# Moving three elementwise jobs of a state-space layer from GpSimd to VectorE, and one convolution tap to ScalarE

## The reference

```
zxbcdt = rms_norm(h, norm_w) @ in_w
z, xbc, dt = split(zxbcdt, [2048, 2048 + 3072])
xbc = silu(causal depthwise conv of 4 taps(xbc) + conv_b)
xs, bm, cm = split(xbc)                      # 32 heads of 64; 4 groups of state 128
dt = softplus(dt + dt_bias);  a_cum = cumsum(dt * a) within chunks of 128
y = sum_j (c_i . b_j) * exp(a_cum_i - a_cum_j) * x_j * dt_j   (j <= i)
y = (y + d_skip * xs) * silu(z)
y = group_norm(y) * gnorm_w @ out_w
```

## Time and profile before

| | |
|---|---|
| median of 3 runs | 1514.42 us (1511.16 to 1514.44) |
| the profiled execution | 1517.64 us, its span 1515.8 us |
| TensorE busy | 1302.9 us (86%), 9346 products |
| VectorE busy | 784.4 us (52%) |
| ScalarE busy | 558.1 us (37%) |
| GpSimd busy | 159.3 us (11%) |
| mean granted TensorE clock | 0.885 of full speed |
| chain that ended last | TensorE 69%, VectorE 11%, DMA 6%, ScalarE 6% |

### The profile page before, as it was taken

The page is one execution under the profiler, slowest core; times in us unless marked ns, Lnnn a source line. Parts: engine busy times, 40 slices in busy tenths (PEclk is TensorE's granted clock), DMA queues, the critical chain, the costliest instruction groups (busy, mean ns, idle before and its releaser), DMA issues.

```text
span 1515.8 us, 21867 instructions
## 1 busy us (share of the span) xinstructions
PE 1302.9 (86%) x9346; PEld 1156.6 (76%) x9346; DVE 784.4 (52%) x1328; ACT 558.1 (37%) x884; POOL 159.3 (11%) x121
## 2 busy tenths in 40 slices
PE   5899697799989998974858999978879888886797
PEld 4787376688868887973848999978867688775697
DVE  0178112944444446480526664358976554547544
ACT  2221513111110005121425553354456754476635
POOL 0101000000000000000000000116635300031000
PEclk8999798889979999556879999979999889899888
DMA  9977478547655454289543555613433234342131
GB/s 302 338 244 254 134 139 248 170 171 271 247 184 176 167 184 156 95 161 233 179 120 125 191 185 183 193 57 114 136 101 95 84 113 137 111 139 84 56 113 55
DMA packets 207029, 244.39 MB, mean 161 GB/s; under 512 B 30596, under 2 KB 191572, under 8 KB 202708
## 3 DMA queue, kind: packets, MB, share of 16 engines
q1 hardware_dynamic: 191752, 183.08, 40.2%
q0 software_dynamic: 10880, 41.95, 8.1%
q10 hardware_dynamic: 4300, 17.96, 3.0%
HBM read 224.16 MB, written 18.81 MB: 160 GB/s over the span
## 4 chain that ended last, share of the span: by engine, by line
PE 69%; DVE 11%; DMA 6%; ACT 6%; SPq 4%; issue 3%; POOL 0%; ACTq 0%; DVEq 0%
PE ps L1256 18%; PE ps L1249 10%; PE ps L1251 9%; PE ps L1253 9%; PE ps L1549 4%; PE ps L1481 3%; PE ps L1304 2%; PE ps L1334 2%; DVE ada_w L2303 2%; DMA ring<-in_w_fc 2%; DMA ring<-k_dram 2%; PE ps L1277 1%; PE ps L1485 1%; PE ps L1462 1%; SPq L664 1%
## 5 line engine op out<-in xcount | busy, mean ns | idle before, releaser
L1249 PE MATMUL ps<-sq_rounded,w_high 128*128 128x256 f32 x960 | 282.6, 294 | 28.7 <-DVE hT_rounded L1846 12.1
L1253 PE MATMUL ps<-sq_rounded,ring_rounded 128*128 128x256 f32 x960 | 275.4, 287 | 0.0
L1839 DVE TENSOR_TENSOR ring_rounded<-ring,w_high 128x1024 fp32r<-128x1024 f32 x152 | 186.7, 1270 | 102.0 <-ACT w_high L800 101.9
L1251 PE MATMUL ps<-hT_rounded,w_high 128*128 128x256 f32 x832 | 239.2, 288 | 0.0
L800 ACT ACTIVATE w_high<-ring 128x1024 fp32r<-128x1024 f32 x176 | 176.0, 1048 | 118.2 <-PE ps L1253 97.2
L1249 PEld LDWEIGHTS ps<-sq_rounded,w_high 128*128 128x128 f32 x960 | 188.8, 197 | 37.5 <-issue 33.2
L1256 PE MATMUL ps<-hT,ring 128*128 128x256 f32 x832 | 193.5, 392 | 7.7 <-DMA ring<-in_w_fc 6.1
L1256 PEld LDWEIGHTS ps<-hT,ring 128*128 128x128 f32 x832 | 161.6, 197 | 38.0 <-issue 15.2
L1253 PEld LDWEIGHTS ps<-sq_rounded,ring_rounded 128*128 128x128 f32 x960 | 188.7, 197 | 0.0
L1251 PEld LDWEIGHTS ps<-hT_rounded,w_high 128*128 128x128 f32 x832 | 164.4, 198 | 0.2
L1249 PE MATMUL ps<-more_rounded,w_high 128*128 128x256 f32 x448 | 126.3, 282 | 0.7 <-issue 0.7
(11 more groups left out here) (378 smaller groups left out, 2047.6 us busy)
## 6 DMA issues: line engine op xcount, KB each, us to landing
ring<-in_w_fc SPq DMA_DIRECT2D x64, 1024.0 KB, 5.4
ada_w<-in_ada_w POOLq DMA_DIRECT2D x27, 1024.0 KB, 7.4
ring<-in_ssm_in_w SPq DMA_DIRECT2D x20, 1024.0 KB, 5.3
ada_more<-in_ada_w POOLq DMA_DIRECT2D x13, 1024.0 KB, 7.6
ring<-in_w_in SPq DMA_DIRECT2D x12, 1024.0 KB, 8.3
we_dram<-we_t ACTq DMA_DIRECT2D x8, 1024.0 KB, 3.9
ca_dram<-more ACTq DMA_DIRECT2D x8, 1024.0 KB, 6.0
ring<-we_dram SPq DMA_DIRECT2D x8, 1024.0 KB, 4.8
```

What stands on the lines that cost most here:

```text
L1249: nc.tensor.matmul(out, high[:, k, columns], x_high, start=start, stop=False, skip_group_check=True)
L1251: nc.tensor.matmul(out, high[:, k, columns], x_low, start=False, stop=False, skip_group_check=True)
L1253: last = nc.tensor.matmul(out, low[:, k, columns], x_high, start=False, stop=stop, skip_group_check=True)
L1839: nc.vector.tensor_tensor(rounded(w), w, w_high[:, c % 2, ks], ALU.subtract)\
```

## The change

- `SPLIT_LO` has VectorE make the low parts of xbc as well. They are placed in VectorE's queue: block 0 ahead of the norm of the layer, block m+1 ahead of `convolve(m)`, z_0 so ahead of `convolve(11)`. At unit 0 the place is behind the wait for the dt products.
- The tap that needs no shift (tap 3) goes to ScalarE: two instructions per unit read PSUM, multiply by the tap and write `convolved`, between the copy into `padded` and the signal `xbc_copied`. VectorE's `convolve` then has three taps, six multiply-adds on `convolved`.
- `weigh` and the gate move to VectorE. weigh(0) and weigh(1) stand ahead of the loop; in iteration t the order is: low part of z_(t/2+1) where t is even, skip(t), segments(t+2), gate(t), and for 1 <= t < 15 weigh(t+1).
- GpSimd keeps only the transfers of the modulation weights and the swaps in the attention layer.

```diff
-SPLIT_LO = {"glu": "vector", "fc1_1": "vector", "fc2_1": "vector", "xbc": "gpsimd", "z": "vector",
+SPLIT_LO = {"glu": "vector", "fc1_1": "vector", "fc2_1": "vector", "xbc": "vector", "z": "vector",
...
-            for b in split_order:
-                if split_low[b][0] == "gpsimd":
-                    for half in range(2):
-                        pool.wait_ge(w_high_ready, 2 * split_place[b] + half + 1)
...
-            weigh(0)
-            weigh(1)
-            for t in range(Z_TILES):
-                pool.wait_ge(zs_ready, t // 2 + 1)
-                pool.wait_ge(y_skipped, t + 1)
-                nc.gpsimd.tensor_tensor(xs[:, t], xs[:, t], zs[:, t], ALU.mult).then_inc(y_gated, 1)
-                if t + 2 < Z_TILES:
-                    weigh(t + 2)
...
-                nc.scalar.activation(padded[:, m % 4].rearrange("p (k n) -> p k n", k=2)[:, :, 3:3 + T], ps,
-                                     ACT.Copy).then_inc(xbc_copied, 1)
+                nc.scalar.activation(padded[:, m % 4].rearrange("p (k n) -> p k n", k=2)[:, :, 3:3 + T], ps, ACT.Copy)
+                if m >= 2:
+                    act.wait_ge(xbc_ready, m - 1)
+                for i in range(2):
+                    tile = 16 + 2 * m + i if m < 4 else 2 * (m - 4) + i
+                    ins = nc.scalar.activation(convolved[:, m % 2, T * i:T * i + T], ps[:, i], ACT.Copy,
+                                               scale=col("ssm_conv_w_2", 72 + tile))
+                ins.then_inc(xbc_copied, 1)
...
+            lower_to(first_block["xbc"] + 1)
             split_norm(5, "ssm_norm_w_2", "xbc")
...
-                for tap in range(4):
+                for tap in range(3):
...
+                lower_to(first_block["xbc"] + m + 2)
                 convolve(m)
...
+            def weigh(t):
+
+                dve.wait_ge(seg_exp, t + 1)
+                s = seg[:, t % 2]
+                nc.vector.tensor_tensor(s, s, cb[:, t // 4].unsqueeze(1).to_broadcast([P, 2, SEG]), ALU.mult)\
+                    .then_inc(seg_weighed, 1)
...
             weigh_by_dt(6)
             weigh_by_dt(7)
+            dve.wait_ge(cb_ready, SSM_GROUPS)
+            weigh(0)
+            weigh(1)
             for t in range(Z_TILES):
...
                 if t + 2 < Z_TILES:
                     segments(t + 2)
+                dve.wait_ge(y_skipped, t + 1)
+                dve.wait_ge(zs_ready, t // 2 + 1)
+                nc.vector.tensor_tensor(xs[:, t], xs[:, t], zs[:, t], ALU.mult).then_inc(y_gated, 1)
+                if 1 <= t < Z_TILES - 1:
+                    weigh(t + 1)
```

More of the change, by code:

```diff
@@ L192, in split_plan @@
     starts = sorted((b, name) for name, b in first_block.items())
-    counts = {"vector": 0, "gpsimd": 0}
+    counts = {"vector": 0}
     for i, (start, name) in enumerate(starts):
@@ L199, in split_plan @@
             counts[SPLIT_LO[name]] += 1
-            low[b] = (SPLIT_LO[name], counts[SPLIT_LO[name]])
+            low[b] = counts[SPLIT_LO[name]]
     return order, place, low
@@ L299, in program @@
         w_low_vector = sem("w_low_vector")
-        w_low_gpsimd = sem("w_low_gpsimd")
         a_high = sem("a_high")
@@ L1240, in block_products @@
                     if split and k // 4 == waited:
-                        engine, count = split_low[b]
-                        pe.wait_ge(w_low_vector if engine == "vector" else w_low_gpsimd, 2 * count - 1 + waited)
+                        pe.wait_ge(w_low_vector, 2 * split_low[b] - 1 + waited)
                         waited += 1
@@ L1834, in lower_to @@
                     b = split_order[c]
-                    for half in range(2) if split_low[b][0] == "vector" else ():
+                    for half in range(2):
                         dve.wait_ge(w_high_ready, 2 * c + half + 1)
@@ L2290, in convolve @@
                 dve.wait_ge(xbc_copied, m + 1)
-                if m >= 2:
-                    dve.wait_ge(xbc_ready, m - 1)
                 src = padded[:, m % 4].rearrange("p (k n) -> p k n", k=2)
-                for tap in range(4):
+                for tap in range(3):
                     for i in range(2):
@@ L2298, in convolve @@
                         dst = convolved[:, m % 2, T * i:T * i + T]
[L2299 to L2302, removed]
+                        if tap:
+                            behind(1)
                         ins = nc.vector.scalar_tensor_tensor(out=dst, in0=src[:, i, tap:tap + T], scalar=w, in1=dst,
                                                              op0=ALU.mult, op1=ALU.add)
-                        if tap == 3 and i == 1:
+                        if tap == 2 and i == 1:
                             ins.then_inc(xbc_conv, 1)
```

## The result

The changed kernel takes 1529.8 us (median of 4 runs, 1527.5 to 1532.1) against 1514.4 us before; the ratio is 1.0109, its 95% interval 1.0084 to 1.0133. It is slower by 15 us, where 1527 us were forecast. The profiled execution took 1529.9 us, its span 1528.0. One more execution of the kernel before took 2132.6 us; it does not enter the ratio.

The account below looks back on a forecast made before the run. Ahead of z1 TensorE waits on VectorE and GpSimd; the z loop has no idle time. Terms -9.0 (xbc stage) -6.7 (up to z1) +16.3 (z-loop wait) +12.5 (clock) = +13.1 us on 1514.4: 1527 us, range 1511 to 1537.

Parts of the forecast that it names:

- dt products to block 3: Start of the xbc stage: VectorE's first low halves come later, so block 3 starts at about 1040.4, against 1039.1.
- block 3 to X: Rest of the xbc stage, X being block 11's end: blocks follow one another, 55.7 us for blocks 3 to 11.
- X to z_1, without the clock: From block 11's end to z1: the 5.8 us wait for z0's low half goes; gain 6.7 us (5 to 8).
- z loop, the wait: Second contraction at S+4.65, not S+1.86 (S: even contraction's start); 2.8 us more per pair, loss 16.3 us (12 to 20).
- z loop and first pair, the clock: TensorE's clock falls to 1.2 GHz in nearly every z pair; loss 12.5 us (0 to 18).
- some 4 us cold, 2 us lost: Each clock fall in a z pair: some 4 us at the low clock, costing half of that busy time, 2 us.
- Rival 1: Clock stays at 2.4 GHz in the z pairs; sum +0.6, 1515 us; chance 0.17.
- The row at 1166.2: Profile row before the change: clock at 1.2 GHz from 1166.2 although TensorE had idled only some 0.4 us.
- Rival 2: Wait before the second contraction shorter (2.0 us a pair), clock kept; sum -7, 1507 us; chance 0.10.
- Rival 3: VectorE bounds the xbc stage too, so the gain there is 4 to 5 us; 1532 us; chance 0.11.
- the signs named beforehand: Include xbc unit ends 5.7 to 5.9 us apart, seven 2.7 us weighing waits, z pairs 12 to 15 us, clock near 0.8.

Follow-up runs that it names:

- six fillers: Changed kernel plus six unused 256-column products on TensorE in each of six waits before an odd contraction (blocks z_1 to z_6); 1516.5 us, ratio 1.0027.

## Why the prediction was right, step by step

The steps by the traces, with the forecast beside them:

| step | forecast | measured | from |
|---|---|---|---|
| dt products to block 3 | +1.3 | +0.9 | 27.9 - 27.0 |
| block 3 to X | -10.3 | -11.2 | 55.5 - 66.7 |
| X to z_1, without the clock | -6.7 | -6.9 | 16.9 - 21.7, less 2.1 |
| z loop, the wait | +16.3 | +15.7 | six fillers against before, 18.3 - 2.6 |
| z loop and first pair, the clock | +12.5 | +19.9 | 15.2 + 2.6 + 2.1 |
| sum | +13.1 | +18.5 | 226.8 - 208.3 |

**The xbc stage** went as worked out. TensorE waited 2.04 us for block 1, where 2.0 were expected between the dt products and 1020.8, and 2.67 us for block 2. Taps cost 0.83 us where 0.85 was taken, the loop stayed under TensorE's pace, and blocks followed one another without a gap. 10.3 us were won by X, 9.0 forecast; the slack of 0.6 us I had kept for weighing by dt wasn't needed. Between block 3 and X the kernel before has 5.8 us of waits and 7.4 us at 1.2 GHz, the changed kernel neither: part of what moving the low halves won is clock as well.

**Up to z_1.** contract(0) starts at X+11.1 in the trace, as forecast to the tenth. The pair behind it took 5.8 us instead of 3.7, because the clock fell in it; that is the 2.1 us counted with the clock (1.7 forecast). The wait of 5.8 us for z_0's low part is gone, as said.

**The wait in the z loop** was right in its mechanism and its size: the second contraction at S+4.62 (S+4.65 forecast), 2.69 us idle in six pairs and 1.92 in the last. The weighing takes 0.95 us where 0.88 was taken, and it starts 0.33 us after the gate where 0.35 was taken. The last pair's wait did disappear behind ScalarE's work: from the last contraction to ssm_out it is 12.9 us, where before it was 14.3. The pair of z_6 paid the full 2.69 us, not the 2.2 that I gave it. The eighth wait, ahead of contract(0), is in X to z_1. The term came out at 15.7 us, as a residual of stage lengths.

**The clock** is the term that was mis-sized: 19.9 us against 12.5, above its bound of 18. The step that failed is "some 4 us cold, 2 us lost". A fall lasted over 6.5 us, not 4, and in the pair shown covered the second spread and most of the block: 29 products in 6.5 us at the low clock, where 4 us hold 37 at the high one.

**The median** came to 1529.8 us, 2.8 us over the forecast, although the stage sum was 5.4 us over it. In the profiled execution that is the head start of 5.7 us ahead of the layer, which I can't put down to the change; the second run of the same kernel (+20.8 us) had less of it. So the closeness of the first median is in part luck, and 18 us is the better value for the change.

**The rivals.** Rival 1 (clock kept) is out: the clock fell in every pair. The row at 1166.2 was the better guide than the rule of the Trainium skill that the prediction cites ("TensorE: Matmul & The Clock Gate", section "HAM oscillation"), which speaks of longer idle gaps. The trace does not agree with that rule: 2.69 us of idle time between small products was enough here each time. Rival 2 needed waits under 2.2 us; they were 2.69. Rival 3 (VectorE bounds the xbc stage) is out, with units 5.60 us apart, even with four taps. Of the signs named beforehand three were off a little. The four pairs without a group norm (after z_1, z_2, z_3 and z_5) lasted 14.0 to 16.6 us where 12 to 15 stood, and the clock was 0.74 where "near 0.8" stood, both for the same reason as the clock term; unit ends were 5.60 us apart, or 6.05 with turned tiles, where 5.7 to 5.9 stood.

## What to carry to other kernels

When work moves to another engine, write out the order of that engine's queue between the two instructions that matter, and ask which of the moved ones stands behind a wait on the very consumer that it feeds. Here VectorE had time for all of it (the gain with the same instructions in another order is 1.3%), but weigh(t+1) stood behind skip(t), which waits for contract(t). And price a recurring wait of TensorE by what the clock does after it too: here the seven waits, 18 us together, brought 15 us of slow products with them.

## What the runs showed of the hardware that I had not expected

A full-precision product (f32 operands, 256 columns) stands twice in the trace: twelve were 24 products and 5.45 us, 0.45 us each, where a product of the rounded kind takes 0.117 us (48 in 5.6 us). And in the pair of z_2 the clock fell not in the idle stretch but after it, while TensorE was busy with contractions and spreads: it was 1.00 at 1129.5 to 1134.8 and 0.50 from 1136.5. That isn't so in every pair. In the pair of z_3 it fell just before the wait ended, and the second contraction takes 1.13 us in place of 0.66:

```profile
1150.29 1.13 PE L1614 MATMUL ps<-ada_more,more 128*64 128x256 f32 x4 [2.69 <-DVE ada_more L2361]
```

Filling the idle 2.7 us with six large products kept it at 1.00 for 34 us, over the same contractions and spreads. What makes the clock fall, the idle time or the small products with it, these runs don't separate. A wait of 2.69 us was followed by a fall each time; a wait of 1.1 us ahead of contract(0) was followed by one in two runs and not in two others.
